# Encoder layer with state-space scan, attention and 32 routed experts on one core: decay terms behind the mask product, other orders at the router's tail and the first experts, a second GpSimd drain, and products of constants ahead of waits

## The chip, the cores and the metric

The kernel runs on one core of one Trainium2 chip. The metric is the device time of one execution in microseconds (us), the median of several runs. The core has five engines that run side by side and meet at semaphores: PE (TensorE: matmuls and transposes, into eight PSUM banks), DVE (VectorE), ACT (ScalarE), POOL (GpSimd, which here also issues the software DMAs: gathers and scatters of rows) and SP (SyncE, which issues the weight loads). PE's clock has two levels, 1.2 and 2.4 GHz; the profile gives the granted clock of a stretch as a share of the full one.

## The reference

One encoder layer on 1024 tokens: two sequences of 512 with shared weights and 1024 channels.

```python
h = rms_norm(x)
P = h @ W_in                      # columns shared among three parallel head groups
x += W_out @ [ssd_heads(P), neighbourhood_attention(P), multiscale_pool(P)]
x += memory_cross_attention(rms_norm(x), rms_norm(mem))
x += hier_moe(rms_norm(x))

# ssd_heads: chunks of 128 tokens, once forward and once backward
seg = cs[:, :, :, None] - cs[:, :, None, :]        # cs = cumsum(dt * a)
decay = exp(where(tri, seg, -inf))
y_diag = einsum('bclgn,bcsgn,bclsgr,bcsgrp->bclgrp', C, B, decay, x * dt)
states = einsum('bclgn,bclgr,bclgrp->bcgrpn', B, decay_end, x * dt)
# y += C @ (state carried into the chunk) * exp(cs);  y = rms_norm(y * silu(z))

# hier_moe: top-1 of 4 groups, in it top-2 of 8 experts
e_id, gates = router(xt)                           # 1024 tokens x 2
for e in range(32):
    hb = silu(xb @ w_e_gate[e]) * (xb @ w_e_up[e])   # rows sorted by expert
    y[tokens of e] += (hb @ w_e_down[e]) * gate
```

## The kernel before

All matrices are fp32. To keep their accuracy each is split into a high and a low part: ACT rounds the high part (L1405: `Wh`, `hTh`, `ghi`, `dhi`, `xgH`), DVE subtracts the low one (L1778 `Wl`, L1806 `hTl`, L1761 `egl`, L2148 `edl`, L2143 `xgL`), and PE makes three matmuls for each product (`three`, L953 to L955), with 512 moving columns at a time.

`timeline()` (L62 to L152) writes one list of steps: `("w", u, q)` is a quarter of the weights of one projection, `("hT", ...)` the transposes of a normed tile, `na1`, `na2` and `nav` the neighbourhood attention, `z` the gate projection, `convT` transposes behind the convolution, `xs2` the transposes of probabilities in the memory attention. Every engine walks the same list in the same order and does its part of each step; a step's place in the list thus is its place in the queues of PE, ACT, DVE and POOL at once. A planner gives the eight banks to the steps in turn; `take` waits until a step's bank is free. `mixed` spreads steps over the quarters of a weight. The file has this once for each sequence s = 0 and 1, in tiles or chunks c of 128 tokens.

The scan. `("sback", s, c)` is the backward state: POOL makes `xw` (L774) from the chunk and its decay weights, PE multiplies (L1096), DVE adds. POOL's part of `z` (the store of the gate to `gate_scratch`, L2388) stands in the same queue. `("sdec", s, c)`: PE makes B times C and multiplies the decay terms `dec` by a strict triangle (L1112), ACT takes exponentials, DVE multiplies masks and decays into `wdt` (L1981 to L1992) and signals `t_done`. `("sy", s, c)`: PE reads the states and `wdt` (L1127 to L1140); DVE sums up y, multiplies it by the gate (L1963), makes the decay terms of the next chunk (`decay_terms(c + 1)`, one product of 128x1024, L1739; the other direction's is POOL's, L2338), waits until ACT and POOL have made the reciprocal root mean square `yrs`, and scales (L1970). `("sout", s, c)`: PE transposes y (L1146). Chunk 3 of a sequence has no next chunk and makes no terms at that place.

The router's tail. For each tile of 128 tokens: `hT ffn`, `router` (PE, L1271), `topk` (DVE, L2082 to L2104: expert numbers, counts `cnt_b`), `rank` (PE, L1278 and L1280: how many earlier tokens chose the expert), `slots` (DVE, L2109 to L2114: one-hot rows of the slots). `place` (PE, L1286; DVE, L2119 to L2123) makes from all slots the row numbers `idh` of each expert, on which POOL gathers the rows `xg`.

The experts. For each of 32: PE transposes the gathered rows (`turn_rows`, L1300), makes gate and up (`gate_up`), transposes the hidden rows (`turn_hidden`, L1322) and multiplies down (`down`, L1335). DVE's order of the first experts is written out by hand: `gate_values` (L2174 to L2187) turns the router's values into gates and splits them in three bf16 parts, PE gathers these to the slots by 17 matmuls (L1343, L1345), `slot_values` (L2193 to L2195) adds them up. SP's `load_down(3)` waits for that, and stands ahead of `load_in(5)` in its queue. POOL gathers the partial sums of a row (`pg<-partial_rows`, L2470) and scatters them back (L2475); the last four experts scatter straight to the outputs (`out_rows`, 8 scatters), after which POOL waits for these, does a test for overlong expert lists (not taken with this data), and ends in the drain that closes the block on each engine (profile line L308).

## Time and profile before

| what | value |
|---|---|
| median of 3 runs | 1071.8 us (1071.31 to 1072.05) |
| profiled execution | 1072.77 us |
| its span | 1070.9 us |
| mean granted clock of PE | 0.961 |
| PE busy | 971.1 us, 91% |
| DVE busy | 774.2 us, 72% |
| ACT busy | 464.9 us, 43% |
| POOL busy | 325.7 us, 30% |
| chain that ended last | PE 67%, DVE 16%, issue 9%, ACT 2%, POOL 2%, DMA 1% |

The span runs from the first to the last instruction of the profiled execution; its own time holds 1.9 us more. "Busy" leaves out waits and the issuing of DMAs by a queue. The chain that ended last is followed back from the last instruction; the share of an engine in it is the time in which its work was what everything else waited for.

### The profile page before, as it was taken

The numbers are of one execution on the slowest core, as the hardware profiler recorded it, in microseconds if no ns is written. First come the engines' busy times: TensorE is split into PE (matmuls) and PEld (weight loads), VectorE is DVE, ScalarE is ACT, GpSimd is POOL, SyncE is SP. The second block draws the span as 40 slices with busy tenths as digits, with TensorE's granted clock in tenths as the row PEclk, the third lists the DMA queues.
The fourth block names the chain that finished last, engine by engine and source line by source line (L and its number), as shares of the span: only waits on it lengthen the run. The fifth ranks groups of instructions, "written<-read, shape, count | busy, mean of one in ns | idle before, by whom it ended". The sixth has DMA issues, their size and how long they took to land.

```text
span 1070.9 us, 13353 instructions
## 1 busy us (share of the span) xinstructions
PE 971.1 (91%) x4709; PEld 757.7 (71%) x4709; DVE 774.2 (72%) x1265; ACT 464.9 (43%) x812; POOL 325.7 (30%) x339
## 2 busy tenths in 40 slices
PE   5998989888889798999998999975999999999993
PEld 4776766556677676668876888864777777777772
DVE  5647776887787577883256677687888888888881
ACT  5234452223344423332034343343666676667650
POOL 2234114321441322210021111014245554555422
PEclk9999998998999898999999999986999999999997
DMA  7232233112232422516020111675899999999981
GB/s 250 70 92 78 92 126 99 60 59 79 80 99 89 157 90 97 159 59 226 20 85 20 40 60 60 260 293 193 334 374 399 402 400 408 408 402 405 406 287 57
DMA packets 63395, 197.38 MB, mean 184 GB/s; under 512 B 16416, under 2 KB 22976, under 8 KB 50912
## 3 DMA queue, kind: packets, MB, share of 16 engines
q1 hardware_dynamic: 43344, 152.73, 38.7%
q0 software_dynamic: 18688, 39.52, 10.4%
q10 hardware_dynamic: 1296, 4.26, 1.0%
q8 instruction: 39, 0.64, 0.2%
q14 instruction: 28, 0.23, 0.1%
HBM read 190.17 MB, written 37.75 MB: 213 GB/s over the span
## 4 chain that ended last, share of the span: by engine, by line
PE 67%; DVE 16%; issue 9%; ACT 2%; POOL 2%; DMA 1%; SPq 0%; ACTq 0%; DVEq 0%; POOLq 0%
PE bank L953 10%; PE bank L954 9%; PE bank L955 9%; PE gu_ps L953 5%; PE gu_ps L955 5%; PE gu_ps L954 5%; PE y_ps L1335 5%; PE xg_ps L1300 3%; DVE Wl L1778 2%; PE bank L1024 2%; PE bank L1227 1%; PE y_ps L955 1%; PE y_ps L954 1%; PE y_ps L953 1%; PE bank L1112 1%
## 5 line engine op out<-in xcount | busy, mean ns | idle before, releaser
L953 PE MATMUL bank<-Wh,hTh 128*128 128x512 f32 x384 | 156.2, 407 | 0.0
L1761 DVE TENSOR_TENSOR egl<-egr,ghi 128x2048 fp32r<-128x2048 f32 x64 | 143.9, 2288 | 14.2 <-ACT ghi L1405 14.2
L954 PE MATMUL bank<-Wl,hTh 128*128 128x512 f32 x384 | 151.0, 393 | 0.0
L955 PE MATMUL bank<-Wh,hTl 128*128 128x512 f32 x384 | 151.0, 393 | 0.0
L1405 ACT ACTIVATE ghi<-egr 128x2048 fp32r<-128x2048 f32 x64 | 119.7, 1934 | 0.0
L953 PE MATMUL gu_ps<-ghi,xgH 128*128 128x512 f32 x256 | 104.3, 408 | 1.4 <-DVE xgL L2143 1.4
L955 PE MATMUL gu_ps<-ghi,xgL 128*128 128x512 f32 x256 | 101.5, 396 | 0.0
L954 PE MATMUL gu_ps<-egl,xgH 128*128 128x512 f32 x256 | 101.0, 395 | 0.0
L953 PEld LDWEIGHTS bank<-Wh,hTh 128*128 128x128 f32 x384 | 73.5, 191 | 16.5 <-issue 2.1
L955 PEld LDWEIGHTS bank<-Wh,hTl 128*128 128x128 f32 x384 | 73.0, 190 | 15.9
L2475 POOL DMA_INDIRECT partial_rows<-pg,idh x28 | 47.5, 1695 | 119.9 <-DVE pg L2168 119.9
L954 PEld LDWEIGHTS bank<-Wl,hTh 128*128 128x128 f32 x384 | 73.2, 191 | 15.0 <-issue 0.5
L2470 POOL DMA_INDIRECT pg<-partial_rows,idh x32 | 68.6, 2143 | 18.1 <-DMA partial_rows<-pg,idh 10.5
L953 PE MATMUL bank<-hTh,Wh 128*128 128x512 f32 (+1 forms) x176 | 70.9, 403 | 0.2 <-DVE Wl L1778 0.2
L1405 ACT ACTIVATE dhi<-edr 128x1024 fp32r<-128x1024 f32 x32 | 33.9, 1060 | 83.6 <-PE y_ps L1335 83.6
L955 PE MATMUL bank<-hTh,Wl 128*128 128x512 f32 (+1 forms) x176 | 69.5, 395 | 0.0
L954 PE MATMUL bank<-hTl,Wh 128*128 128x512 f32 (+1 forms) x176 | 69.3, 394 | 0.0
L1778 DVE TENSOR_TENSOR Wl<-raw,Wh 128x1024 fp32r<-128x1024 f32 (+1 forms) x45 | 59.2, 1320 | 11.2 <-ACT Wh L1405 11.2
L2322 POOL TENSOR_SCALAR ms<-ssq 128x1 f32<-128x1 f32 x28 | 6.6, 237 | 195.8 <-ACT xn_ffn L1468 79.0
L1335 PE MATMUL y_ps<-edr,hbF 128*128 128x512 f32 x128 | 65.4, 592 | 0.0
L2168 DVE SCALAR_TENSOR_TENSOR pg<-y_ps,gate_s,pg 128x1024 f32<-128x1024 f32 x32 | 41.1, 1284 | 26.3 <-PE y_ps L1335 24.2
L953 PEld LDWEIGHTS gu_ps<-ghi,xgH 128*128 128x128 f32 x256 | 49.1, 192 | 11.0 <-DVE xgL L2143 1.8
(328 smaller groups left out, 2092.8 us busy)
## 6 DMA issues: line engine op xcount, KB each, us to landing
egr<-w_e_gate SPq DMA_DIRECT2D x32, 1024.0 KB
egr<-w_e_up SPq DMA_DIRECT2D x32, 1024.0 KB
edr<-w_e_down SPq DMA_DIRECT2D x32, 1024.0 KB, 12.5
raw<-w_in SPq DMA_DIRECT2D x50, 256.0 KB, 3.0
xn<-w_in SPq DMA_DIRECT2D x22, 256.0 KB, 2.9
x_sb<-x_prompt SPq DMA_DIRECT2D x8, 512.0 KB, 6.0
partial_rows<-x_sb ACTq DMA_DIRECT2D x8, 512.0 KB, 2.7
raw<-w_xkv SPq DMA_DIRECT2D x14, 256.0 KB, 3.7
```

The lines of the kernel that those rows point to most:

```text
L953: pe.matmul(dst, ah, bh, start=first, stop=False)
L954: pe.matmul(dst, ah, bl, start=False, stop=False)
L955: return pe.matmul(dst, al, bh, start=False, stop=last)
L1024: last = pe.transpose(b[:, j * P:(j + 1) * P], src[:, f * P:(f + 1) * P], ident[:, :])
L1300: ins = pe.transpose(xg_ps[:, k * P:(k + 1) * P], xg[n % 3][:, k:D:KT], ident[:, :])
L1335: last = pe.matmul(y_ps[:, c], hbF[:, :], edr[n % 4][:, 1, c], start=False, stop=True)
L1405: return act.activation(dst, src, ACT.Copy, **kw)
L1761: tt(egl[n % 4][:, a, :, :], egr[n % 4][:, a, :, :], ghi[n % 2][:, a, :, :].bitcast(F32), ALU.subtract)\
L1778: tt(lo, src, h, ALU.subtract).then_inc(w_low, 1)
L2168: stt(pg[n % 4][:, :], y_ps[:, :], gate_s[:, e:e + 1], pg[n % 4][:, :], ALU.mult, ALU.add)\
L2470: return pool.indirect_dma_start(out=to, out_offset=None, in_=table, in_offset=bass.IndirectOffsetOnAxis(ap=idx, axis=0), bounds_check=bou ...
L2475: return pool.indirect_dma_start(out=table, out_offset=bass.IndirectOffsetOnAxis(ap=idx, axis=0), in_=frm, in_offset=None, bounds_check=bo ...
```

## The change

- In `timeline`: `("sback", s, 3)` stands in the third quarter of z in place of the fourth; the second attention step of tile 1 stands ahead of the transposes of conv 0; `slots` of tiles 5 and 6 stand right behind the last `hT ffn`.
- On DVE `decay_terms(c + 1)` moves from the middle of `sy` to the end of `sdec` of the same chunk.
- `place` copies one half of its bank and reads the other half from PSUM.
- On PE a new function issues matmuls of constants (256 moving columns) into a bank that the next step overwrites, ahead of ten waits: 159 in all.
- At the first experts PE's slot sums stand between `gate_up(1)` and `down(0)`; DVE's second low half of expert 1 stands ahead of `gate_values`, whose last three products (now `split_values`) come behind `rows_low(1)`, and `slot_values` comes behind `hidden(1)`.
- POOL does a `drain()` ahead of the output scatters.

```diff
--- before.py
+++ after.py
@@ -105,10 +105,10 @@
                [act[5], na2[0], u_t[0], u[1], nav[0]]], quarters(u0 + U_XS))
-        mixed([[na1[1], conv[0]], [act[0], conv[1], conv_t[0], na2[1]]], quarters(u0 + U_Z))
+        mixed([[na1[1], conv[0]], [act[0], conv[1], na2[1], conv_t[0]]], quarters(u0 + U_Z))
         tl += [act[1], norm[0], conv[2], conv_t[1], nav[1], act[2], na1[2], norm[1], conv[3], conv_t[2], u_t[1], ("dtv", s)]
         mixed([[z[0], act[3], h_t[0], na2[2], ("dtw", s)], [z[1], h_t[1], norm[2], nav[2], na1[3], ("dt", s)],
-               [z[2], conv_t[3], h_t[2], norm[3], na2[3]], [z[3], ("sback", s, 3), nav[3], ("sback", s, 2), h_t[3]]],
+               [z[2], conv_t[3], h_t[2], norm[3], na2[3], ("sback", s, 3)], [z[3], nav[3], ("sback", s, 2), h_t[3]]],
               quarters(u0 + 5 if s == 0 else U_MK))
@@ -146,8 +146,8 @@
     tl += [("pre", 0), ("xs2", i), ("hT", "ffn", i - 1), ("prl", 0), ("xav", i), ("norm", "ffn", i - 1), ("topk", i - 2),
-           ("router", i - 1), ("topk", i - 1), ("xo", i), ("rank", i - 2), ("rank", i - 1), ("stt", i - 1), ("hT", "ffn", i),
-           ("norm", "ffn", i), ("stt", i), ("slots", i - 2), ("router", i), ("pre", 1), ("topk", i), ("slots", i - 1),
+           ("router", i - 1), ("topk", i - 1), ("xo", i), ("rank", i - 2), ("rank", i - 1), ("stt", i - 1), ("hT", "ffn", i), ("slots", i - 2), ("slots", i - 1),
+           ("norm", "ffn", i), ("stt", i), ("router", i), ("pre", 1), ("topk", i),
            ("rank", i), ("slots", i)]
@@ -685,6 +685,14 @@

+        WARM = {("sback", 0, 2): 8, ("sback", 1, 2): 8, ("xs2", 0): 19, ("convT", 0, 0): 12, ("convT", 1, 0): 12, ("convT", 1, 4): 24,
+                ("rank", NT - 1): 20, ("place",): 12, "rows": 34, "gate": 10}
+
+        def constant_products(pe, to, n):
+
+            for _ in range(n):
+                pe.matmul(to[:, 0:256], ones_r[:, :], tri_r[:, :, :].rearrange("p a b -> p (a b)"), start=True, stop=True)
+
         def take(pe, step, j=0):
@@ -1059,9 +1067,10 @@
                     s, m = step[1], step[2]
+                    b = take(pe, step)
+                    constant_products(pe, b, WARM.get(step, 0))
                     pe.wait_ge(conv_out, 1 + nth("conv", s, m))
                     src = cacc[:, nth("conv", s, m) % 2, :] if m < 4 else bT[:, :]
-                    b = take(pe, step)
                     for c in range(TPS):
@@ -1091,8 +1100,9 @@
                     wait_released(pe, ("convT", s, 4))
+                    b = take(pe, step)
+                    constant_products(pe, b, WARM.get(step, 0))
                     pe.wait_ge(xw_done, 1 + xw_no(s, 1, c))
-                    b = take(pe, step)
                     pe.matmul(b[:, :], btm[:, c, :], xw[:, :], start=True, stop=True).then_inc(is_full(step), 1)
@@ -1133,8 +1143,9 @@
                             .then_inc(is_full(step, 3), 1)
+                    b = take(pe, step, 0)
+                    constant_products(pe, b, WARM.get(step, 0))
                     pe.wait_ge(t_done, 2 * nth("sdec", s, c) + 2)
-                    b = take(pe, step, 0)
                     for h in range(SSD_H):
@@ -1229,6 +1240,7 @@
                     i = step[1]
+                    constant_products(pe, take(pe, step), WARM.get(step, 0))
                     pe.wait_ge(prob_done, 1 + sm_no(2, i))
@@ -1275,13 +1287,15 @@
                     b = take(pe, step)
+                    constant_products(pe, b, WARM.get(step, 0))
                     pe.matmul(b[:, 0:NE], ones_b[:, :], csum[:, i, :], start=True, stop=False)
...
                 elif kind == "place":
+                    b = take(pe, step)
+                    constant_products(pe, b, WARM.get(step, 0))
                     pe.wait_ge(slots_done, NT)
-                    b = take(pe, step)
                     for j in range(2 * NT):
@@ -1293,6 +1307,8 @@

+                if n == 0:
+                    constant_products(pe, xg_ps, WARM["rows"])
                 pe.wait_ge(xg_ld[n % 3], 16 * (n // 3 + 1))
@@ -1303,6 +1319,8 @@

+                if n == 0:
+                    constant_products(pe, gu_ps[0], WARM["gate"])
                 pe.wait_ge(xg_low, 2 * n + 2)
@@ -1335,19 +1353,24 @@

+            def slot_sums():
+
+                pe.wait_ge(vals_done, 1)
+                for j in range(2 * NT):
+                    pe.matmul(r_ps[:, 0:3 * NE].rearrange("p (a b) -> p a b", a=3), oneh_p[:, j, :], idv2[:, j, :, :],
+                              start=j == 0, stop=j == 2 * NT - 1)
+                pe.matmul(r_ps[:, 4 * NE:5 * NE], ones_b[:, :], csum[:, NT, :], start=True, stop=True).then_inc(vals_full, 1)
+
             turn_rows(0)
...
             turn_rows(1)
-            pe.wait_ge(vals_done, 1)
-            for j in range(2 * NT):
-                pe.matmul(r_ps[:, 0:3 * NE].rearrange("p (a b) -> p a b", a=3), oneh_p[:, j, :], idv2[:, j, :, :],
-                          start=j == 0, stop=j == 2 * NT - 1)
-            pe.matmul(r_ps[:, 4 * NE:5 * NE], ones_b[:, :], csum[:, NT, :], start=True, stop=True).then_inc(vals_full, 1)
             for n in range(1, NE):
...
                 gate_up(n)
+                if n == 1:
+                    slot_sums()
                 down(n - 1)
@@ -1961,9 +1984,6 @@
                         tt(y1[:, :], y1[:, :], zg[:, :], ALU.mult).then_inc(y_done, 1)
-                        if c < TPS - 1:
-                            dve.wait_ge(t_done, 2 * k + 2)
-                            decay_terms(c + 1)
                         dve.wait_ge(yrs_done, k + 1)
@@ -1991,6 +2011,9 @@
                     ins.then_inc(t_done, 1)
+                    if c < TPS - 1:
+                        dve.wait_ge(t_done, 2 * k + 2)
+                        decay_terms(c + 1)
                 elif kind == "sout":
@@ -2116,9 +2139,9 @@
                     dve.wait_ge(hn_st, 16 * NT)
-                    link(dve.tensor_copy(r_id[:, :, :].rearrange("p a b -> p (a b)"), pb(step)[:, 0:2 * NE]))
+                    link(dve.tensor_copy(r_id[:, 0, :], pb(step)[:, 0:NE]))
                     ts(hrow2[:, :], r_id[:, 0, :], 0.0, 5000.0, ALU.is_equal, ALU.mult)
-                    link(stt(hrow[:, :], r_id[:, 1, :], float(P), r_id[:, 0, :], ALU.mult, ALU.add))
+                    link(stt(hrow[:, :], pb(step)[:, NE:2 * NE], float(P), r_id[:, 0, :], ALU.mult, ALU.add))
                     stt(idh[:, :], hrow[:, :], -1.0, hrow2[:, :], ALU.add, ALU.add).then_inc(ids_done, 1)
@@ -2181,6 +2204,9 @@
                 link(tt(gsp[:, 2, :, :], g_res[:, 0, :, :], gsp[:, 1, :, :], ALU.subtract))
+
+            def split_values():
+
                 flat = lambda v: v.rearrange("p c t -> p (c t)")
@@ -2219,11 +2245,11 @@
             gate_low(1, 0)
+            gate_low(1, 1)
             gate_values()
             hidden(0)
-            gate_low(1, 1)
             rows_low(1)
-            slot_values()
+            split_values()
             down_low(1)
@@ -2232,6 +2258,8 @@
                 hidden(n)
+                if n == 1:
+                    slot_values()
                 add_rows(n - 1)
@@ -2517,6 +2545,7 @@
                     gather_sums(n + 1)
+            pool.drain()
             for n in range(NE - 4, NE):
```

## Rows read from the trace of the kernel before

**Rows 1.** The profile page: busy time of two engines, and two of the costliest groups.

```profile
PE 971.1 (91%) x4709; PEld 757.7 (71%) x4709; DVE 774.2 (72%) x1265; ACT 464.9 (43%) x812; POOL 325.7 (30%) x339
...
L2475 POOL DMA_INDIRECT partial_rows<-pg,idh x28 | 47.5, 1695 | 119.9 <-DVE pg L2168 119.9
...
L2470 POOL DMA_INDIRECT pg<-partial_rows,idh x32 | 68.6, 2143 | 18.1 <-DMA partial_rows<-pg,idh 10.5
```

**Rows 2.** Windows of 25 and 10 us: busy us of each engine, clock, DMA.

```profile
186.00:211.00 25.00, 20.34 (x94) 14.64 (x93) 21.26 (x53) 6.49 (x18) 8.08 (x9) 0.93 0.19 54
730.00:740.00 10.00, 7.06 (x20) 5.62 (x21) 6.42 (x14) 6.07 (x5) 8.17 (x7) 0.50 0.63 171
825.00:850.00 25.00, 25.00 (x115) 19.16 (x114) 22.20 (x22) 15.48 (x23) 12.23 (x8) 1.00 1.01 402
```

**Rows 3.** Instructions of the last line and of the first: POOL's drains (ns).

```profile
L308 POOLq DRAIN  x1: 8892/8892/8892, 1061.8 to 1061.8; - x1
...
L2595 POOLq DRAIN  x1: 173/173/173, 0.3 to 0.3; - x1
```

**Rows 4.** Timeline of POOL, 1030 to 1071: start, us, what, idle before.

```profile
1031.91 1.01 POOL L2470 DMA_INDIRECT pg<-partial_rows,idh  x1 [2.10 <-DMA partial_rows<-pg,idh]
1048.34 1.00 POOL L2475 DMA_INDIRECT y_prompt<-pg,idp  x1 [15.42 <-issue]
...
1058.41 0.97 POOL L2475 DMA_INDIRECT y_sample<-pg,ids  x1 [0.30 <-issue]
```

**Rows 5.** Timeline of POOL, 150 to 166.

```profile
154.70 1.05 POOL L774 TENSOR_TENSOR xw<-x_sb,wst 128x512 f32<-128x512 f32 x1
```

**Rows 6.** Timeline of PE at L1096, in the two sequences.

```profile
155.86 1.10 PE L1096 MATMUL bank<-xw,x_sb 128*128 128x512 f32 x2 [0.40 <-issue]
...
161.81 2.05 PE L1096 MATMUL bank<-xw,x_sb 128*128 128x512 f32 x2 [3.96 <-issue]
...
363.99 2.05 PE L1096 MATMUL bank<-xw,x_sb 128*128 128x512 f32 x2 [4.71 <-issue]
```

**Rows 7.** Timeline of PE, 712 to 762.

```profile
714.91 1.09 PE L1024 MATMUL bank<-ident,x_sb 128*128 128x128 f32 x8 [1.19 <-DVE x_sb L2068]
716.83 3.60 PE L1271 MATMUL bank<-router_ws,hf 128*128 128x40 f32 x16 [0.83 <-ACT hf L1405]
...
723.39 0.21 PE L1280 MATMUL bank<-cnt_b,tri_b 128*128 128x32 bf16 x1 [2.92 <-DVE cnt_b L2099]
...
731.53 1.94 PE L1300 MATMUL xg_ps<-ident,xg 128*128 128x128 f32 x8 [4.83 <-DMA xg<-ffn_rows,idh]
...
740.17 0.63 PE L953 MATMUL gu_ps<-ghi,xgH 128*128 128x512 f32 x1
740.60 0.46 PE L954 MATMUL gu_ps<-egl,xgH 128*128 128x512 f32 x1
...
747.80 1.94 PE L1300 MATMUL xg_ps<-ident,xg 128*128 128x128 f32 x8 [2.52 <-DVE xgL L2143]
...
759.87 0.47 PE L953 MATMUL gu_ps<-ghi,xgH 128*128 128x512 f32 x1
```

**Rows 8.** Timeline of PE behind two other waits.

```profile
282.33 0.66 PE L1066 MATMUL bank<-ident,x_sb 128*128 128x128 f32 x4 [3.73 <-DVE x_sb L1869]
...
566.85 1.97 PE L1237 MATMUL bank<-ident,prob 128*128 128x128 f32 x8 [2.76 <-DVE prob L1757]
```

**Rows 9.** Who waited for the decay terms of L1739 (us, times).

```profile
  PE bank L1112: 17.1, 5
```

**Rows 10.** Timeline of DVE at L1970, 186 to 282.

```profile
199.25 0.62 DVE L1970 TENSOR_SCALAR y<-y,yrs 128x256 f32<-128x256 f32 x2 [0.90 <-POOL yrs L2323]
...
267.33 2.29 DVE L1970 TENSOR_SCALAR y<-y,yrs 128x256 f32<-128x256 f32 x2 [2.04 <-POOL yrs L2323]
```

**Rows 11.** The software gathers of L2470: from issue to landing.

```profile
DMA to landing us min/median/max: 3.5/11.3/14.9
```

## The prediction

> **What bounds the kernel now.** I read the busy table first, then the windows, then the waits of single lines, and the last 40 us by themselves. The busy table [rows 1] shows TensorE (PE) at 91% and VectorE (DVE) at 72% of a span of 1070.9 us. The share is an average over stages with different limits, so the windows [rows 2] come next. In the steady expert loop PE is busy 25.00 of 25 us at clock 1.00; no edit touches that loop, and it can only begin or end at another time. In the window that begins at 186 us PE is busy 20.34 and DVE 21.26: there DVE works nearly all the time and PE stands in between, its clock falling to 0.93. From 730 to 740 us, at the first experts, PE is busy 7.06 of 10 at clock 0.50, its lower level (1.2 of 2.4 GHz). Last, behind the last output, GpSimd (POOL) is in one drain of 8892 ns [rows 3]: nothing else runs, so each microsecond of it is one of the kernel's. The change therefore acts in four places: the end of a sequence's projections, the scan (186 to 282 and 390 to 480 us), the way into the experts (715 to 760), and the end.
>
> The profiled execution took 1072.8 us for a span of 1070.9, 1.9 around it, and lies 1.0 above the median of 1071.8; I carry that 1.0 over.
>
> **H, the second drain.** What can a drain at the end be doing for 8.9 us? Not waiting for data: the last scatter was issued by 1059.4 [rows 4], POOL passed its wait on the outputs, and the drain begins only at 1061.8. The drain at the kernel's start, before any software DMA, took 173 ns [rows 3]. Between the two POOL issued its software DMAs, 32 + 28 in two groups of the expert loop alone [rows 1]. So I take the 8.7 us as work that grows with the DMAs issued since the drain before. The new drain stands ahead of the last 8 scatters. Of at least 60 + 8 DMAs 8 would remain: 8.7 × 8/68 = 1.0, and the end shrinks by 7.7; the other gathers of the loop (32 for xg) and the stores of the mixer make the share of 8 about half of that, 0.5, and the gain 8.2. I take **−8.2**. What hides the new one: POOL is idle for 15.42 us ahead of its first scatter at 1048.34 [rows 4], from 1032.9; 8.9 us end at 1041.8, 6.5 to spare. Queued behind it are only the scatters. Bounds: −8.7 and 0.
>
> In a sentence of its own: the Trainium skill ("VectorE: DVE Perf Modes", section "The DRAIN you can't avoid") says the drains of a program's preamble and postamble are about 12 ns, constant, on all five engines. This trace shows 8892 ns for POOL's, so it disagrees there; by that rule no drain's cost can be moved, and H would be worth nothing, which is the first rival below.
>
> **A, the backward state product of chunk 3 moved ahead of z[3].** At PE it now comes in front of the 24 matmuls of z[3] (0.23 us from start to start at full clock, 5.5 us), and it needs xw. POOL makes xw only after the store of z[2], at 154.70 to 155.75 [rows 5]; the edit leaves that store where it was. Before, z[3]'s matmuls lay between, and PE waited 0.40 at 155.86 [rows 6]. Without them PE reaches the wait 5.5 us earlier, at 155.86 − 0.40 − 5.5 = 150.0, and stands 5.8 us. In return z[3] and the attention values (L1200) then lie in front of the next such product, so its wait of 3.96 at 161.81 (4.71 at 363.99) goes; its 8 constant products cost 0.9 and hold the clock up for the 8 transposes behind it, which ran at half speed (some 0.9 back). 5.8 − 0.4 − 3.96 = +1.4, and by the same steps 5.8 − 0.4 − 4.71 = +0.7 for the second sequence; a chain of DVE behind it makes that a little more. The earlier attention transposes (B; 12 products) shift some 0.6 of DVE's work out of the way. I take **+2.3** for both. Bounds: −8.3 (both later waits go, and nothing new stands) and +11.6 (twice 5.8, nothing back).
>
> **C and E, products ahead of a wait.** A product here moves 256 columns, half of the 512 of the expert matmuls, whose starts lie 0.43 us apart at half clock (740.17 and 740.60 [rows 7]) and half of that, with the clock twice as high, at full: 0.11 or 0.21 each. Ahead of the wait of 3.73 us at 282.33 stand 24 (2.7 us at full clock), ahead of the 2.76 at 566.85 stand 19 (2.1) [rows 8]. Both fit. They take nothing from the wait; what they give is the clock behind it. At 566.85 eight transposes take 1.97, where eight of the same kind take 1.09 at 714.91 [rows 7]; eight more follow: 0.8 to 0.9 for each eight, **−1.6**. At 282 as much work follows at half clock (eight matmuls of L1181, four of L1077), and PE then runs on without a wait: **−1.7**. Bounds 0 and −2 each, at 0 where DVE is the next to be waited for.
>
> **D, decay terms behind the mask product.** PE waited for them at L1112, 17.1 us in 5 waits [rows 9]. All of that goes. But who is late next? DVE's work is the same 1.22 us per chunk, 6 chunks, only later. In its old place it lay inside DVE's wait for the root mean square that POOL returns: 0.90 left of it at 199.25, and 2.04 at 267.33 where a chunk has no decay terms [rows 10]. So in six chunks DVE's idle grows by 1.14. PE's next need of DVE is y, which follows that very wait; it comes at the same time as before. So where DVE sets the pace each chunk is 1.14 us longer, and PE's wait only moves from L1112 to the output transposes. From 186 us on DVE's idle (25 − 21.26 in that window) is such round trips, so the first sequence pays most of 3 × 1.14: 2.9. In the second PE is nearer the pace, and I take half: 1.6. **+4.5**. Bounds: six times the whole product and round trip, 6 × (1.22 + 1.14) = +14.2; and −17.1, if PE set the pace.
>
> **F and G, the way into the experts.** The slots of tiles 5 and 6 (some 1.0 us each on DVE) leave the chain from the router's result to the placement; the first lay ahead of an operation that PE delayed anyway, and the second ahead of a rank that arrives 0.4 later, so the indices come 0.4 earlier. The 20 products ahead of rank(7) start at half clock, behind sixteen router matmuls of 3.60 us in place of 1.9, with 2.92 us of wait to fill [rows 7]: 20 × 0.21 = 4.2, less as the clock returns; an overrun of about 0.9. The 34 products (3.8 us) in the wait of 4.83 at 731.53 bring the eight transposes back from 1.94 to 1.09: −0.8. Gate-up of expert 0 has 13 matmuls at 0.43 in place of 0.23: −2.6. Then DVE: expert 1's second low half now stands ahead of the gate values, so the rows of expert 1 are split some 4.5 us earlier, and the wait of 2.52 that PE has for them at 747.80 moves up with them and stays, as long as PE's work ahead of it is as much shorter. The slot sums (17 matmuls, 0.85), formerly within a wait, now lie between gate-up(1) and down(0) and cost 0.85. Together gate-up of expert 2 starts at about 755.4 in place of 759.87: **−4.5** (0.4 and 0.8 and 2.6, the 2.52 and some 1.1 of half clock behind it, less 0.9 for the overrun and 0.85 for the sums, is 5.7; I keep 1.2 back for DVE, on which both splits wait). The load of down weights 3 waits for these sums and comes 6 us later, but its consumer is two experts away; SP's gate load of expert 5 queues behind it with 10 us to spare. Bounds −7 (no overrun, nothing of the 0.85) and −2 (the clock stays at half).
>
> In a sentence of its own: the Trainium skill ("TensorE: Matmul & The Clock Gate", section "Part 4: PE-mode transpose") says transposes do not count as PE work for the clock the way matmuls do. By it the transposes right behind the products could lose the clock again, and E and G's 0.8 would go: 2.4 us, inside the bounds.
>
> **Sum.** +2.3 − 1.7 + 4.5 − 1.6 − 4.5 − 8.2 = −9.2. 1072.8 − 9.2 = 1063.6 for a profiled execution, **1062.6** for the median (1071.8 − 9.2).
>
> **Rivals.**
> 1. The drain's cost can't be moved (it belongs to the end of the program whatever came before). For: its place, with nothing outstanding. Against: 173 ns at the start. 1062.6 + 8.2 = 1070.8. 18 in 100.
> 2. The scan gains: PE was the pace-setter there. For: PE waits of 17.1 us, clock 0.93. Against: DVE 21.26 of 25 and every idle of it a round trip. A quarter of 17.1 = −4.3 in place of +4.5: 1053.8. 16 in 100.
> 3. Slower: the new drain waits for the gather in flight and costs its time again. A software DMA of this kind lands 3.5 to 14.9 us after issue [rows 11]; the last gather is issued at 1031.91. At 13.5 it lands at 1045.4, the drain ends at 1054.3, and eight scatters at 1.28 us end at 1064.5 in place of 1059.4: +5.1. With a drain of unchanged length at the end the sum is −1.0 + 5.1, 1075.9. It decides once the new drain ends past 1049.2 (1059.4 − 10.2). Against: the idle before it is wide, and no drain in this trace shows a wait. 7 in 100. If the end also shrinks, 1067.7: part of my range.
> 4. The waits that I see for sback(3) come out in full, +11.6 in place of +2.3: 1071.9. For: PE's order is fixed. Against: the work behind it fills the later wait. 6 in 100.
>
> My own forecast has 53 in 100.
>
> **Range and chances.** Low 1053.5 (rival 2), high 1071.3 (rival 1 with half a microsecond); beyond them I leave about 2 in 10. 0.2% is 2.1 us, about what a measurement of this kernel can tell from no change. Faster takes my case, rival 2, the mild form of 3 and part of rival 1: 0.79. Same: most of rivals 1 and 4, 0.13. Slower: rival 3 and the bad sides of A and D, 0.08.
>
> **What would show it.** H: a POOL drain near 1033 of some 8 us and one under 1.2 at the end. D: no wait at L1112, a wait of about 2.0 for yrs ahead of L1970 in every chunk, and new PE waits at L1146. A: one PE wait near 5 us ahead of the first L1096, and none at the second. C, E: clock full behind 282 and 566. F, G: clock 1.00 from 731, gate-up(2) some 4.5 earlier against the placement's start. I am wrong if the drain at the end keeps its length, if the scan's windows shrink, or if PE stands for expert loads behind the late down load.

## The result and the profile after

The changed kernel is slower: 1074.55 us (median of 10 runs, 1071.84 to 1076.65) against 1071.23 (10 runs, 1068.38 to 1074.06), ratio 1.003 with an interval of 1.0015 to 1.0044, so +3.2 us. I had forecast −9.2, and the range ended at 1071.3. The profiled execution took 1074.31 us with a span of 1072.3, near its median; the one of before lay 1.5 above its own, so the two traces differ by 1.4 in span where the medians differ by 3.3.

The letters A to H are those of the prediction. The end went as forecast. Here are the new drain and the last one, which was 8892 ns [rows 3] (durations in ns):

```profile
L2548 POOLq DRAIN  x1: 9771/9771/9771, 1040.5 to 1040.5; - x1
...
L308 POOLq DRAIN  x1: 702/702/702, 1071.4 to 1071.4; - x1
```

POOL's timeline, which answers to [rows 4]:

```profile
1040.71 1.00 POOL L2498 DMA_INDIRECT pg<-partial_rows,idh  x1 [3.45 <-DMA partial_rows<-pg,idh]
1057.62 1.01 POOL L2503 DMA_INDIRECT y_prompt<-pg,idp  x1 [15.90 <-DMA y_sample<-partial_rows]
...
1067.99 0.97 POOL L2503 DMA_INDIRECT y_sample<-pg,ids  x1 [0.30 <-issue]
```

The new drain takes 9771 ns, so the cost has moved and not gone. It ends at 1050.3, 7.4 us ahead of the first scatter, and the gap ahead of that scatter is as wide as before: the new drain is hidden. But that scatter starts at 1057.62 in place of 1048.34. Everything ahead of the end is 9.3 us later; less 8.2 for the drain, and with 0.3 more from the first scatter to the last, that is the span's +1.4. The loss lies elsewhere. I matched the same instructions of PE in the two traces and took the difference of their starts:

| matmul, its start before | later by (us) | in the stretch |
|---|---|---|
| L1195, 138.94 | +0.4 | behind the attention step (B) |
| first of the weights behind both state products, 170.40 | +4.5 | A: +4.1 |
| L1066, 282.33 | +7.9 | D: +3.5 |
| L953, 286.86 | +6.3 | C: −1.7 |
| L1195, 340.37 | +5.7 | (−0.6, put down to no edit) |
| weights behind both state products, 372.17 | +10.2 | A: +4.4 |
| L1146, 479.51 | +13.7 | D: +3.6 |
| L1249, 570.64 | +13.5 | E: −0.2 |
| gate-up of expert 2, 759.87 | +9.6 | F, G: −3.9 |
| first output scatter, 1048.34 | +9.3 | |

The moved state product (A) in PE's timeline, beside [rows 6]:

```profile
156.31 2.05 PE L1106 MATMUL bank<-xw,x_sb 128*128 128x512 f32 x2 [5.90 <-POOL xw L782]
...
165.31 1.22 PE L694 MATMUL bank<-tri_r,ones_r 128*128 128x256 f32 x8
166.37 1.02 PE L1106 MATMUL bank<-xw,x_sb 128*128 128x512 f32 x2
...
174.88 0.50 PE L961 MATMUL bank<-Wh,hTh 128*128 128x512 f32 x1 [2.49 <-DVE Wl L1801]
```

The stand is the forecast's 5.8, and the later wait of 3.96 is gone. PE then catches up, since it runs at full clock here where it ran at half before: at 169.0 us it is 1.9 later than before. Then comes a new wait of 2.49 for DVE. Its releaser's queue, DVE:

```profile
167.43 4.06 DVE L1972 TENSOR_TENSOR S_b<-S_b,edec 64x256 f32<-64x256 f32 x2 [1.19 <-PE bank L1106]
171.53 0.85 DVE L1978 TENSOR_TENSOR S_b<-S_b,bank 64x256 f32<-64x256 f32 x2
172.41 1.29 DVE L1829 TENSOR_TENSOR hTl<-bank,hTh 128x512 fp32r<-128x512 f32 x2
173.62 1.22 DVE L1801 TENSOR_TENSOR Wl<-xn,Wh 128x1024 fp32r<-128x1024 f32 x1
```

and POOL in the same stretch:

```profile
168.29 1.06 POOL L782 TENSOR_TENSOR xw<-x_sb,wst 128x512 f32<-128x512 f32 x1
169.29 1.90 POOL L2366 TENSOR_TENSOR dec<-la,tri_r 128x1024 f32<-128x1024 f32 x1
```

Two products of 64x256 take 4.06 us on DVE, more than four times what they take elsewhere (0.87 at 182.13), and they end at 171.5, 0.3 us behind POOL's two products (171.2). They are not waiting for a semaphore: the profile counts the time as work. An operation of DVE was held while POOL computed.

The scan (D). DVE's scaling at L1990 answers to [rows 10], PE's L1122 to [rows 9]:

```profile
205.13 0.62 DVE L1990 TENSOR_SCALAR y<-y,yrs 128x256 f32<-128x256 f32 x2 [2.03 <-POOL yrs L2351]
232.66 2.04 DVE L1990 TENSOR_SCALAR y<-y,yrs 128x256 f32<-128x256 f32 x2 [2.03 <-POOL yrs L2351]
256.80 0.63 DVE L1990 TENSOR_SCALAR y<-y,yrs 128x256 f32<-128x256 f32 x2 [2.05 <-POOL yrs L2351]
```

```profile
  DVE y L1983: 12.0, 4
```

The wait for yrs is 2.03 to 2.06 in each chunk, as forecast. PE's wait at the decay matmuls did not go: 12.0 of 17.1 us stay (11.8 ahead of matmuls, 0.2 ahead of a weight load), now for DVE's sum of y (L1983), and PE waits another 2.1 for the same sum at L1114. The planner gives sdec(c + 1) the bank that sy(c) had, and that sum is what frees it. Decay terms that are ready early are of no use to matmuls that have no bank.

The places of C and E, beside [rows 8], and the way into the experts, beside [rows 7]; PE:

```profile
287.40 3.03 PE L694 MATMUL bank<-tri_r,ones_r 128*128 128x256 f32 x24
290.26 0.60 PE L1075 MATMUL bank<-ident,x_sb 128*128 128x128 f32 x4
...
580.62 1.09 PE L1249 MATMUL bank<-ident,prob 128*128 128x128 f32 x8 [0.50 <-DVE prob L1780]
...
732.21 3.91 PE L694 MATMUL bank<-tri_r,ones_r 128*128 128x256 f32 x20
735.93 0.25 PE L1291 MATMUL bank<-csum,ones_b 128*128 128x32 bf16 x1
...
744.64 1.06 PE L1316 MATMUL xg_ps<-ident,xg 128*128 128x128 f32 x8
...
769.50 0.48 PE L961 MATMUL gu_ps<-ghi,xgH 128*128 128x512 f32 x1
```

Behind the products the clock is full where it was at half (eight transposes in 1.09 and 1.06 for 1.97 and 1.94). Products can themselves fall into half clock: the 20 at 732.21 take 3.91, where 24 take 3.03 at full clock. Gate-up of expert 2 starts 3.9 us earlier against what lies ahead.

One wait here was in no term of mine. The placement needs the last tile's rows to have landed in memory (`hn_st`), and in this kernel that comes last:

```profile
739.52 0.19 DVE L2142 COPY r_id<-bank 128x32 f32<-128x32 f32 x1 [2.10 <-DMA ffn_rows<-xn]
```

The placement's matmuls were done by 738.5; the copy starts 5.89 us behind the issue of that store. In the kernel before it started 6.97 behind it and waited for PE. An edit that brings ranks, slots or matmuls forward gains no more than this landing leaves.

### The profile page after: what moved, and what is told of

It reads as the page before. It is cut to its first block, busy times and chain, and to the rows that moved or that the text cites. A ratio compares the mean times of both kernels' runs of the same rounds, so it can differ in the third digit from the quotient of the medians.

```text
span 1072.3 us, 13669 instructions
## 1 busy us (share of the span) xinstructions
PE 986.6 (92%) x4868; PEld 772.9 (72%) x4868; DVE 776.8 (72%) x1265; ACT 465.0 (43%) x812; POOL 326.8 (30%) x339
## 4 chain that ended last, share of the span: by engine, by line
PE 43%; DVE 6%; issue 3%; DMA 2%; POOL 1%; ACT 1%; SPq 0%; ACTq 0%; DVEq 0%; POOLq 0%
PE gu_ps L963 5%; PE bank L961 5%; PE gu_ps L961 5%; PE bank L962 5%; PE gu_ps L962 5%; PE bank L963 5%; PE y_ps L1353 4%; PE xg_ps L1316 2%; PE bank L1238 2%; PE y_ps L963 1%; PE y_ps L961 1%; PE y_ps L962 1%; PE bank L1032 1%; DMA y_sample<-partial_rows 1%; DVE hTl L1829 1%
## 5 line engine op out<-in xcount | busy, mean ns | idle before, releaser
L2498 POOL DMA_INDIRECT pg<-partial_rows,idh x32 | 70.9, 2214 | 14.5 <-issue 8.9
L963 PEld LDWEIGHTS gu_ps<-ghi,xgL 128*128 128x128 f32 x256 | 48.3, 189 | 10.5
```

Source lines behind the costliest of these rows:

```text
L963: return pe.matmul(dst, al, bh, start=False, stop=last)
L2498: return pool.indirect_dma_start(out=to, out_offset=None, in_=table, in_offset=bass.IndirectOffsetOnAxis(ap=idx, axis=0), bounds_check=bou ...
```

## The experiments

Each ratio is to the kernel before, run on the same chip. A difference from the kernel before is the ratio's, times 1071 us. Differences between two other kernels are given by their medians or by their ratios; by the intervals of the ratios such a difference is uncertain by 2 to 3 us.

**1. The moved state product undone in the changed kernel.**

```diff
-               [z[2], conv_t[3], h_t[2], norm[3], na2[3], ("sback", s, 3)], [z[3], nav[3], ("sback", s, 2), h_t[3]]],
+               [z[2], conv_t[3], h_t[2], norm[3], na2[3]], [z[3], ("sback", s, 3), nav[3], ("sback", s, 2), h_t[3]]],
```

> The changed kernel with one edit undone: the backward state product of chunk 3 stands in the fourth quarter of z again, as before; all the rest stays. Theory: the move costs 4.1 us in the first and 4.4 in the second sequence (by the starts of the same matmuls in the two traces), because TensorE stands 5.9 us for xw, runs z[3] at half clock, and VectorE's state update then meets GpSimd's decay product and takes 4.06 us in place of 1.60. So this kernel should be 8.5 below the changed one, 1066 us, and 5 below the one before. Rival: the lateness would have come anyway, since VectorE is the bound there; then undoing it gives under 3 us (1072 or more).

Measured: 1064.57, ratio 0.9939 (0.9918 to 0.9961). That is 9.8 us under the changed kernel by the ratios; the theory's 8.5 is inside the uncertainty, the rival is out.

**2. The decay terms back in the wait for yrs.**

```diff
                         tt(y1[:, :], y1[:, :], zg[:, :], ALU.mult).then_inc(y_done, 1)
+                        if c < TPS - 1:
+                            dve.wait_ge(t_done, 2 * k + 2)
+                            decay_terms(c + 1)
                         dve.wait_ge(yrs_done, k + 1)
...
                     ins.then_inc(t_done, 1)
-                    if c < TPS - 1:
-                        dve.wait_ge(t_done, 2 * k + 2)
-                        decay_terms(c + 1)
```

> The changed kernel with one edit undone: VectorE makes the decay terms of the next chunk in its wait for the root mean square again. Theory: the move costs 3.5 and 3.7 us in the two scans, 7.2, so this kernel takes 1067.4; the waits for yrs shrink from 2.03 to 0.90 in six chunks (6.8 us). Rival: TensorE was the bound and gained from the move; then this kernel is slower than the changed one, by up to 4 us.

Measured: 1069.6, ratio 0.9985 (0.9968 to 1.0001), 4.8 us less than the changed kernel by the ratios, where the theory had 7.2. The rival is out. DVE's waits are back at 0.9, PE waits for `dec` again, and the kernel is faster with PE's wait than without it:

```profile
205.05 0.62 DVE L1993 TENSOR_SCALAR y<-y,yrs 128x256 f32<-128x256 f32 x2 [0.90 <-POOL yrs L2351]
```

```profile
204.21 6.03 PE L1122 MATMUL bank<-dec,strict 128*128 128x512 f32 x8 [4.58 <-DVE dec L1762]
```

**3. Both undone**, everything else of the change kept.

> Both undone, the rest of the change kept. Theory: the two costs lie in different stretches and add up: 1074.5 - 8.5 - 7.2 = 1058.8, 12.4 below the kernel before, which is what the drain (8.2), the router's tail and first experts (4.2) and the products at 282 and 566 (2.0) give, less what the attention step in front of the conv transposes costs. Rival: the gain is the drain alone (8.2), the products cost as much as they give: 1063.

Measured: 1058.06 (1056.28 to 1060.28), ratio 0.9879 (0.9851 to 0.9907). By the ratios this is 16.2 us under the changed kernel, and the two single costs sum to 14.6: they add up within the uncertainty. It is the lowest median of all kernels here.

**4. The drain alone.**

```diff
+            pool.drain()
             for n in range(NE - 4, NE):
                 out_rows(n)
```

> The kernel before with the second GpSimd drain and nothing else. Theory: a drain's time grows with the software DMAs issued since the last one, and the new one lies in 15 us of idle time; 8.2 us less than before, 1063.0, with a last drain of 0.7 us. Rival: only the place of the cost moves and the scatters start later or the interval holds 0; 1068 or more.

Measured: 1062.9, ratio 0.9925 (0.990 to 0.995), 8.0 us. The new drain takes 10829 ns and the last one 702. So do all last drains of the kernels with the second drain, and the three kernels without it (before, 9 and 10) have 8892. A drain's time goes with the software DMAs since the drain before it; how much of the new one's 10829 is a wait for the gather issued beside it is not shown.

**5. GpSimd's first decay terms later.**

```diff
                 elif kind == "sback" and step[2] > 1:
                     decayed(pool, step[1], 1, step[2] - 1, per_head, heads)
-                    if step[2] == 2:
-                        if step[1]:
-                            wait_full(pool, ("sdec", step[1] - 1, TPS - 1), 3)
-                        decay_terms(0)
...
                 elif kind == "sdec":
...
+                    if c == 0:
+                        if s:
+                            wait_full(pool, ("sdec", s - 1, TPS - 1), 3)
+                        decay_terms(0)
```

> The changed kernel, but GpSimd makes the first decay terms of a sequence (a product of 128x1024) not right behind the state product's operand but at the head of its part of sdec(s, 0), some 5 us later. Theory: with the moved state product VectorE's update of S_b (two products of 64x256, 4.06 us in place of 1.60) is held while GpSimd works on that product; without it the update takes 1.0 to 1.6 us again and the wait of 2.49 at the next weights goes: up to 2.4 us per sequence, 1069.7 to 1072. Rival: the update is slow because of something else (the store of the attention, the operand's product, or its own data); then it stays near 4 us and the time near 1074.5.

Measured: 1076.82, ratio 1.0041 (1.0024 to 1.0057), by the ratios 1.2 us slower than the changed kernel, which is not clear of noise; the forecast gain did not come. DVE's timeline:

```profile
168.70 2.21 DVE L1972 TENSOR_TENSOR S_b<-S_b,edec 64x256 f32<-64x256 f32 x2 [1.19 <-PE bank L1106]
170.94 0.85 DVE L1978 TENSOR_TENSOR S_b<-S_b,bank 64x256 f32<-64x256 f32 x2
```

The update takes 2.21 in place of 4.06: without the product of 1.90 the hold is 1.85 shorter, and PE's wait at the next weights is 0.65 in place of 2.49, which is what the theory says of the mechanism. The time was a miss: the terms now came too late for the first decay matmuls, which wait 4.08 and start at 181.34 in place of 177.75 (1.3 of that lay ahead of the stand already). What was won was lost there.

**6. Products inside the new stand.**

```diff
-        WARM = {("sback", 0, 2): 8, ("sback", 1, 2): 8, ...
+        WARM = {("sback", 0, 3): 44, ("sback", 1, 3): 44, ("sback", 0, 2): 8, ("sback", 1, 2): 8, ...
```

> The changed kernel with 44 products of constants (5 us at full clock) ahead of the moved state product of chunk 3 in each sequence, inside TensorE's new stand of 5.9 us. Theory: z[3]'s 24 matmuls then run at full clock, 7.0 us in place becomes 5.5, so TensorE is 1.5 us earlier there in each sequence; but VectorE's update is what is late next, so 1 to 3 us in all: 1071.5 to 1073.5. Rival: the half clock behind the stand is the main cost of the move, and its removal gives back most of the 8.5: 1068.

Measured: 1077.74, ratio 1.0043 (1.0021 to 1.0066), no better than the changed kernel. PE:

```profile
151.71 5.52 PE L694 MATMUL bank<-tri_r,ones_r 128*128 128x256 f32 x44
157.76 1.13 PE L1106 MATMUL bank<-xw,x_sb 128*128 128x512 f32 x2 [0.53 <-POOL xw L782]
...
174.75 0.50 PE L961 MATMUL bank<-Wh,hTh 128*128 128x512 f32 x1 [2.48 <-DVE Wl L1801]
```

z[3] runs at full clock, and the wait at the next weights is 2.48 as before. But this execution was 1.5 us late already where the stand begins (+1.5 at 130 us), and the weights start at 174.75 in place of 174.88: from the stand to there PE is 1.6 us faster, since DVE's and POOL's work behind z[3] moved up with it. In this trace 2.4 us were won up to the router, and 3.6 lost behind it: the rows landed 7.96 us behind their store in place of 5.89, and the 34 products took 5.80 in place of 4.31:

```profile
740.74 0.19 DVE L2142 COPY r_id<-bank 128x32 f32<-128x32 f32 x1 [4.17 <-DMA ffn_rows<-xn]
```

Whether the products have to do with that landing is not shown. The regained clock did not take DVE's hold away, and the median shows no gain.

**7. Both moves and the attention step undone**, products kept.

```diff
-        mixed([[na1[1], conv[0]], [act[0], conv[1], na2[1], conv_t[0]]], quarters(u0 + U_Z))
+        mixed([[na1[1], conv[0]], [act[0], conv[1], conv_t[0], na2[1]]], quarters(u0 + U_Z))
```

> Both moves undone as in the kernel at 1058.1, and the attention step of tile 1 behind the conv transposes again too. Theory: that edit (with its 12 products) was worth 0.5 to 1.0 us behind its wait and gave it back within 30 us, so the time is 1058 within 1.5. Rival: it costs 1.6 us per sequence (the drift between 109 and 139 us), then 1055.

Measured: 1058.47, ratio 0.986 (0.9838 to 0.9881): the same as experiment 3. Where the 12 products stand ahead of that wait, the step's place is worth nothing that this can measure.

**8. Both moves undone, no products at all** (the loop of `constant_products` runs over 0).

> Both moves undone, and none of the 159 products of constants is issued; orders of the tail and of the first experts and the drain stay. Theory: products give 1.7 at 282, 0.3 to 0.5 at 566 and about 3 (0.8 + 2.6, less an overrun) at the first experts: 1058.1 + 5 = 1063. Rival: the reordering alone gives the 4 us at the first experts and the products next to nothing: 1059 to 1060.

Measured: 1058.34, ratio 0.9869 (0.9849 to 0.9888). A miss of mine, and the rival's case: with the attention step moved, 159 products make no difference that this can measure (experiment 16 has another case). The two traces show where it goes. Without products PE reaches the same matmuls up to 1.9 us later or 2.4 earlier, so the products cost time at some places and save it at others, and at gate-up of expert 2 the kernel without them is 0.5 us ahead (752.12 against 752.60). In the tail, with products and then without:

```profile
722.28 5.80 PE L694 MATMUL xg_ps<-tri_r,ones_r 128*128 128x256 f32 x34 [1.91 <-DVE hrow L2146]
727.92 1.06 PE L1316 MATMUL xg_ps<-ident,xg 128*128 128x128 f32 x8
```

```profile
726.66 1.95 PE L1316 MATMUL xg_ps<-ident,xg 128*128 128x128 f32 x8 [5.97 <-DMA xg<-ffn_rows,idh]
```

Here 34 products, 3.8 us at full clock, took 5.80, since half of them fell into half clock (starts 0.21 apart, then 0.12). The transposes behind them start 1.3 us later than without products, though POOL issued the gather 0.6 earlier (722.32 against 722.91).

**9. The decay terms moved in the kernel before**, nothing else.

> The kernel before with the decay terms behind the mask product and nothing else. Theory: the cost of this edit stands by itself: six yrs waits grow from 0.90 to 2.03 (6.8 us), and of TensorE's 17.1 us of waits at the decay matmuls all but some 5 come back as a wait for the bank that VectorE's sum of y releases. 4 to 7 us slower than before. Rival: within the changed kernel the cost came from its meeting with the moved state product; alone it is within 2 us of the kernel before.

Measured: 1078.89, ratio 1.007 (1.0044 to 1.0096), +7.5 us. PE at the first decay matmuls:

```profile
200.03 5.37 PE L1112 MATMUL bank<-dec,strict 128*128 128x512 f32 x8 [4.14 <-DVE y L1960]
```

Nobody waits for `dec` any more, and PE waits 4.14 for the bank where it waited 4.66 for `dec`. The cost stands by itself, and the rival is out.

**10. The state product moved in the kernel before**, nothing else.

> The kernel before with the state product of chunk 3 in the third quarter of z and nothing else. Theory: the same 8 to 10 us as when it is undone in the changed kernel, so about 1081. Rival: the earlier attention step and the products of the change made it worse (they hold VectorE's order); alone it costs under 4 us.

Measured: 1074.58, ratio 1.0034 (1.0015 to 1.0053), +3.6 us. Against 9.8 in the changed kernel this is the rival's side: some 6 us come from a meeting of this edit with another. Experiments 13 to 15 follow that up.

**11. As 8, and the slots of tiles 5 and 6 in their old places** (F without its shorter copy).

> The kernel at 1058.3 without any products and both moves undone, and now the slots of tiles 5 and 6 in their old places too. Theory: the slots' new place is worth 0.4 to 1 us (the indices come that much earlier): 1059. Rival: it is the main part of the 5 us that the drain does not explain; then 1062.

Measured: 1058.65, ratio 0.9887 (0.9867 to 0.9907): 1.9 us slower than kernel 8 by the ratios, 0.3 by the medians, not clear of noise. In the traces the old places end the placement's matmuls 1.8 us later against the store of the last rows, and the copy behind them starts only 0.7 later (6.79 us behind the store for 6.13), since in kernel 8 it waits for the rows to land.

**12. As 8, and the first experts in their old order.**

```diff
             turn_rows(1)
+            slot_sums()
...
             gate_low(1, 0)
-            gate_low(1, 1)
             gate_values()
+            split_values()
             hidden(0)
+            gate_low(1, 1)
             rows_low(1)
-            split_values()
+            slot_values()
...
```

> The kernel at 1058.3 without any products and both moves undone, and now the first experts in their old order (slot sums behind turn_rows(1), gate values with their three products ahead of hidden(0), second low half of expert 1 behind it). Theory: the new order brings gate-up(1) 3 to 4 us forward, all of which reaches the steady loop: 1061.5 to 1062.5. Rival: the steady loop is bound by its loads (402 GB/s), so an earlier start is lost in it: 1059 or less.

Measured: 1061.12, ratio 0.9907 (0.9888 to 0.9926): the order gives 2.8 us by the medians, 4.1 by the ratios, without any product. The steady loop keeps it.

**13. The changed kernel without the eight products ahead of sback(s, 2).**

```diff
-        WARM = {("sback", 0, 2): 8, ("sback", 1, 2): 8, ("xs2", 0): 19, ...
+        WARM = {("xs2", 0): 19, ...
```

> The changed kernel without the 8 products of constants ahead of the state product of chunk 2 (one group in each sequence). Theory: these 8 hold that product back by 0.9 us, so VectorE's update of S_b begins at 168 in place of 167 to 171, but ahead of GpSimd's two products: it takes 0.87 us as in the kernel where the move stands alone, and the hold falls on the next weights' subtraction, at 1.6 us in place of 3.2. 2 to 4 us less than the changed kernel, 1071 to 1072.5. Rival: the eight have nothing to do with it; 1074.5.

Measured: 1070.34, ratio 0.9991 (0.9976 to 1.0007), 4.2 us under the changed kernel. DVE and then POOL:

```profile
167.84 0.87 DVE L1972 TENSOR_TENSOR S_b<-S_b,edec 64x256 f32<-64x256 f32 x2 [0.23 <-PE bank L1106]
168.75 0.85 DVE L1978 TENSOR_TENSOR S_b<-S_b,bank 64x256 f32<-64x256 f32 x2
...
170.84 2.82 DVE L1801 TENSOR_TENSOR Wl<-xn,Wh 128x1024 fp32r<-128x1024 f32 x1
```

```profile
169.65 1.06 POOL L782 TENSOR_TENSOR xw<-x_sb,wst 128x512 f32<-128x512 f32 x1
170.66 1.91 POOL L2366 TENSOR_TENSOR dec<-la,tri_r 128x1024 f32<-128x1024 f32 x1
```

The update starts 1.8 us ahead of POOL's products, where it started 0.9 ahead of them in the changed kernel, slips in and takes 0.87. The hold falls on the next weights' subtraction instead, 2.82 in place of 1.22: 1.6 where it was 3.2. Between the two, DVE's L1829 runs beside POOL's first product and takes its usual 1.29:

```profile
169.63 1.29 DVE L1829 TENSOR_TENSOR hTl<-bank,hTh 128x512 fp32r<-128x512 f32 x2
```

It reads one of its inputs from a bank; the two operations that were held read both from SBUF (the on-chip memory of the tiles that are in no bank), as POOL's products do.

**14 and 15. The changed kernel without any products, and the same with the state product in its old place.**

> The changed kernel with none of its 159 products, all orders as changed. Theory: as with both moves undone (1058.3 without, 1058.1 with products), the products give nothing in sum, and those ahead of chunk 2's state product cost 2 to 4 us with the moved one: 1071 to 1072.5. Rival: products and orders do not interact: 1074.5 within 1.

> As the run before it, and the state product of chunk 3 in its old place. The difference between the two is the price of the move without any products. Theory: 3.6 to 6 us as in the kernel where the move stands alone, against 9.9 with the products: 1066.5. Rival: the move costs 8 to 10 us whatever the products do: 1063.

Measured: 1069.47, ratio 0.9987 (0.9971 to 1.0003), and 1064.98, ratio 0.9933 (0.9913 to 0.9954). Without products the move costs 4.5 us (5.8 by the ratios), with them 9.8. And all products together cost the changed kernel 4.6 us, which the eight alone explain (4.2).

**16. The drain, the first experts' order and the shorter copy alone.**

> What is left when all that gave nothing is out: the kernel before with the second drain, the new order of the first experts and the shorter copy at the placement; no products, both moves and the attention step and the slots undone. Theory: 8.2 for the drain and 2.8 for the experts: 1060, and no slower than the kernels at 1058.1 to 1058.6 by more than 1.5. Rival: the slots' order and the attention step carry 2 us that the single runs did not resolve: 1062.

Measured: 1063.78, ratio 0.9912 (0.9891 to 0.9934); the rival's side. It is kernel 11 with the attention step (B) back behind the conv transposes, and the medians differ by 5.1; the ratios, each against its own chip's runs, differ by 2.7, which is not clear of noise. The windows of kernel 11 and then of this one around that step (columns as in [rows 2]):

```profile
100.00:116.00 16.00, 13.52 (x75) 11.19 (x74) 13.97 (x16) 10.78 (x19) 6.51 (x10) 1.00 0.35 109
```

```profile
100.00:116.00 16.00, 12.68 (x57) 10.65 (x56) 13.10 (x15) 10.18 (x20) 6.46 (x10) 0.89 0.26 84
```

and PE in kernel 11, then in this one:

```profile
108.68 0.63 PE L1075 MATMUL bank<-ident,x_sb 128*128 128x128 f32 x4 [2.48 <-DVE x_sb L1892]
```

```profile
109.25 1.09 PE L1075 MATMUL bank<-ident,x_sb 128*128 128x128 f32 x4 [3.33 <-DVE x_sb L1892]
110.13 1.91 PE L1192 MATMUL bank<-ident,prob 128*128 128x128 f32 x8
```

Behind a wait of 3.33 the clock is at half here; behind 2.48 it is not. In the profiled execution of the kernel before the same wait was 3.23 and the clock stayed full (the four transposes took 0.66). Kernel 4 is the kernel before up to its last 40 us; in its profile the wait is 3.23 too, and the clock is at half:

```profile
109.04 1.12 PE L1066 MATMUL bank<-ident,x_sb 128*128 128x128 f32 x4 [3.23 <-DVE x_sb L1869]
```

So this wait sits at an edge, and a single trace shows one of two outcomes. It is also where products can pay. Kernel 7 has the step in the old place as well, but keeps the products; in its trace PE stands 1.83 at this place and the clock is full, and it is 5.3 us faster than kernel 16 (5.6 by the ratios), of which the slots have at most some 2.

## Why the prediction was wrong

**H** held: −8.2 forecast, −8.0 measured alone, the reason as given. The first and the third rival are out; the rule of the Trainium skill named there ("VectorE: DVE Perf Modes", section "The DRAIN you can't avoid") does not hold for POOL's drain: 8892 ns and 702 ns in two kernels that differ in this line. The new drain takes 9771 ns where I expected some 8 us, and is hidden all the same.

**A** is the step that failed: "a chain of DVE behind it makes that a little more. I take +2.3". Measured are +8.5 by the starts and 9.8 when undone. PE's own part was right: the stand of 5.9, the later wait gone, PE 1.9 us late at 169. What stood behind it was not a little. The eight products, which I had priced at 0.9 us of PE with some 0.9 back, held the next state product until POOL was about to start two products (0.9 us ahead of them; 1.8 without the eight), and DVE's update was then held for 3.2 us, in both sequences. Taken alone the move costs 3.6, with all products 9.8, and the eight products account for 4.2 of the difference. In the trace of before the same update took 1.60 at 163.89, already more than the 0.86 of its twin at 177.51; I had not compared them.

**B** I had as a help of some 0.6. With the 12 products its place is worth nothing measurable (7 against 3), without products 2.7 to 5.1 us (16 against 11), of which the smaller figure is not clear of noise. The traces of 11 and 16 differ there in the clock behind a wait that the trace of before did not show as an edge.

**D** was right in mechanism and mis-sized: +4.5 forecast, 4.8 when undone, 7.5 when made alone, 7.1 by the starts. The waits are the forecast's (2.03 to 2.06 for about 2.0), but all six chunks pay, not four: 6 × 1.13 = 6.8. "In the second PE is nearer the pace, and I take half" failed. The sentence "All of that goes" was wrong as well: 12.0 of PE's 17.1 us stayed as a wait for the bank, and 2.1 came up at L1114. Rival 2 is out by experiments 2 and 9.

**C and E** showed the forecast's picture at their places (−1.7, and −1.6 at first) and were worth nothing measurable at the end: E's gain is given back within 4 us of trace at the next wait, C's by the comparison of experiments 3 and 8. The condition that I wrote as a bound, "at 0 where DVE is the next to be waited for", was the case. The transposes right behind the products kept the full clock (1.06 us for eight at 744.64, behind 34 products), so nothing here shows the rule of the Trainium skill ("TensorE: Matmul & The Clock Gate", section "Part 4: PE-mode transpose") at work.

**F and G**: −4.5 forecast, −3.9 by the starts. The parts were others than I said: the order of the first experts gives 2.8 to 4.1 without a product, the slots 0.7 by the traces, 0.3 by the medians, and the 2.6 + 0.8 of clock that I gave to the products nothing measurable (8). I had left out that the placement waits for the last rows to land.

The size of the whole: A's +2.3 was +8.5 by the starts, D's +4.5 was +7.1, E's −1.6 was −0.2. These are 6.2 + 2.6 + 1.4 = 10.2 of the 10.6 between the forecast's −9.2 and the traces' +1.4. Of the rivals' figures rival 3's 1075.9 is nearest to the measured 1074.55, and that is luck: its drain costs nothing where it stands. Rival 4 has the right place (A at +11.6, 1071.9), by another mechanism than the one I gave it.

Open: whether the move without products costs more in one kernel than in another (3.6 alone, 4.5 to 5.8 with the other edits; their intervals overlap), and how much of B's 2.7 to 5.1 is the clock. The fastest kernels are 3, 7, 8 and 11, at 1058.1 to 1058.7: the kernel before with the drain, the new order of the first experts, and either the attention step moved or the products kept.

## What to carry to other kernels

When a wait is removed, list all that the waiting instruction needs, its bank too, and look who frees it: of PE's 17.1 us at `dec` 12.0 were left at the bank, and the kernel was no faster for the rest, while the cover that was taken from DVE's round trip cost 1.13 us in every chunk. Work inside another engine's round trip was free here; moved out, it cost the whole of the trip that it had covered. Filling PE's waits with products gave nothing where another engine or a landing came next in the chain (3 against 8), and some 5 us where it kept the clock up at one edge (7 against 16); and whatever stands ahead of a wait can delay a product just far enough to meet another engine. Before an edit that shifts DVE against POOL, look for DVE operations that take longer than their twins of the same shape.

## What the hardware showed that I had not expected

POOL's last drain takes 8892 ns behind all of the kernel's software DMAs and 702 ns behind the last eight; the drain put ahead of these takes 9771 ns, 10829 in kernel 4.

Some DVE operations stretch while POOL computes, and the profile counts it as busy: two products of 64x256 take 0.87, 1.60, 2.21 or 4.06 us, a subtraction of 128x1024 takes 1.22 or 2.82, and the 4.06 and the 2.82 are longer than their twins by about as much as POOL's products ran beside them (3.2 and 1.6). Taking one of POOL's products away shortened the first (experiment 5), starting it earlier freed it (13). The held ones read both inputs from SBUF; one that read an input from a bank, beside the same product of POOL, took its usual 1.29 (13). POOL can pay too: in the kernel before, where DVE's update started 0.05 us ahead, POOL's two products took 1.27 and 2.08 in place of 1.05 and 1.90. Which operation pays depends on starts a microsecond apart.

PE's clock behind a wait of 3.23 us stayed full in one execution and was at half in another (kernel 4's), with the same instructions up to there.

The rows that POOL stores at the router's end had landed by 5.9 us behind the issue in the changed kernel and by 8.0 us in experiment 6; the gather of the first expert's rows was issued 2 us later for it.
